# Streaming encoder step with a hierarchical mixture of experts: choices and expert blocks joined into one stage

## The reference: what is computed

```
grp_logits = xt @ w_grp + b_grp                    # 4 groups, xt = rmsnorm(x1)
g_sel      = argmax(grp_logits)                    # one group for each row
e_logits   = xt @ w_exp + b_exp                    # 32 experts, 8 in a group
top_val, top_idx = top_k(e_logits of the group, 2) # two experts for each row
weights    = softmax(grp_logits)[g_sel] * softmax(top_val)
for each chosen expert e:                          # w_e1, w_e3: 1024 x 512, w_e2: 512 x 1024
    h = silu(xb @ w_e1[e]) * (xb @ w_e3[e])
    y += (h @ w_e2[e]) * weight
out = x1 + y
```

## Time and profile before

| | |
|---|---|
| median of three runs | 1229.96 us |
| profiled execution, its own time | 1227.32 us |
| its span, first to last instruction | 1225.5 us |
| busy share of the span: PE, DVE, ACT, POOL | 88%, 35%, 29%, 32% |
| moved by DMA | 289.10 MB, of which queue q1 249.40 MB |
| expert matrices | 96 loads of 2048 KB, median 32.4 us from issue to landing |
| mean granted TensorE clock | 0.956 of full speed |

### The profile page before, as it was taken

The page is one execution under the profiler, slowest core; times in us unless marked ns, Lnnn a source line. Parts: engine busy times, 40 slices in busy tenths (PEclk is TensorE's granted clock), DMA queues, the critical chain, the costliest instruction groups (busy, mean ns, idle before and its releaser), DMA issues. The chain is left out here.

```text
span 1225.5 us, 20512 instructions
## 1 busy us (share of the span) xinstructions
PE 1084.5 (88%) x8243; PEld 832.5 (68%) x8243; DVE 428.3 (35%) x988; ACT 354.5 (29%) x748; POOL 391.2 (32%) x428
## 2 busy tenths in 40 slices
PE   5999899899999989999999896888888888887783
PEld 4998898798999877888898673454445444444441
DVE  6698733891111363342323442211211111111116
ACT  6547633352222644453332431000000000000000
POOL 4454458841211443322554101221212112211100
PEclk9999989898988989999999887999999999999996
DMA  7332236255322531114421898999999999999997
GB/s 130 90 83 70 69 83 167 48 158 130 91 74 61 205 103 38 50 53 139 141 79 44 304 425 354 425 428 424 430 425 429 427 429 427 429 427 430 427 427 264
DMA packets 149678, 289.10 MB, mean 236 GB/s; under 512 B 43668, under 2 KB 119028, under 8 KB 132832
## 3 DMA queue, kind: packets, MB, share of 16 engines
q1 hardware_dynamic: 94224, 249.40, 52.4%
q10 hardware_dynamic: 49632, 27.46, 8.3%
q0 software_dynamic: 5744, 11.15, 2.4%
HBM read 269.30 MB, written 26.54 MB: 241 GB/s over the span
## 5 line engine op out<-in xcount | busy, mean ns | idle before, releaser
L492 PE MATMUL bank<-xhi,cv_w_hi 128*128 128x272 f32 x848 | 260.1, 307 | 9.5 <-PEq L135 3.2
L478 POOL TENSOR_TENSOR cv_w_lo<-cv_w_raw,cv_w_hi 128x1024 fp32r<-128x1024 f32 (+1 forms) x69 | 167.9, 2433 | 310.6 <-ACT cv_w_hi L471 291.8
L2559 PE MATMUL bank<-e_w,b_xT 128*64 128x256 f32 x2048 | 231.0, 383 | 24.4 <-DVE b_xT L2588 14.9
L492 PE MATMUL bank<-xhi,cv_w_lo 128*128 128x272 f32 x848 | 251.2, 296 | 0.0
L492 PE MATMUL bank<-xlo,cv_w_hi 128*128 128x272 f32 x848 | 250.4, 295 | 0.0
L2559 PEld LDWEIGHTS bank<-e_w,b_xT 128*64 128x64 f32 x2048 | 147.3, 138 | 98.0 <-DVE b_xT L2588 19.1
L492 PEld LDWEIGHTS bank<-xhi,cv_w_hi 128*128 128x128 f32 x848 | 165.8, 195 | 18.2 <-issue 10.2
L492 PEld LDWEIGHTS bank<-xlo,cv_w_hi 128*128 128x128 f32 x848 | 166.3, 196 | 0.9
L492 PEld LDWEIGHTS bank<-xhi,cv_w_lo 128*128 128x128 f32 x848 | 165.8, 196 | 0.0
L2571 PE MATMUL bank<-e_w,b_hiddenT 128*64 128x512 f32 x512 | 116.9, 598 | 18.9 <-DVE b_hiddenT L2596 18.9
L2524 POOL COPY b_target<-slot_target 128x1 int32 (+1 forms) x31 | 5.5, 178 | 309.0 <-ACT b_y L2581 288.9
(11 more groups left out here) (447 smaller groups left out, 1641.9 us busy)
## 6 DMA issues: line engine op xcount, KB each, us to landing
e_w<-in_w_e SPq DMA_DIRECT2D x96, 2048.0 KB, 32.4
cv_w_raw<-in_w_in ACTq DMA_DIRECT2D x34, 512.0 KB, 4.2
cv_w_raw<-in_w_in SPq DMA_DIRECT2D x18, 512.0 KB, 3.9
cv_w_raw<-in_w_br_b ACTq DMA_DIRECT2D x8, 512.0 KB, 4.1
o_raw<-in_w_out SPq DMA_DIRECT2D x16, 256.0 KB, 3.7
y_rows<-choice_rows SPq DMA_DIRECT2D x8, 512.0 KB, 11.7
g_values_gates<-g_z_stage ACTq DMA_DIRECT2D x12, 272.0 KB, 4.6
f_gates<-g_values_gates SPq DMA_DIRECT2D x2, 1088.0 KB, 8.7
```

The source lines that it names most:

```text
L478: self.k.nc.gpsimd.tensor_tensor(self.wlo[:, s, 0:nk, :], self.raw[:, s, 0:nk, :], self.whi[:, c % OPS, 0:nk, :].bitcast(F32), ALU.subtract)\
L492: last = self.k.nc.tensor.matmul(self.bank(c, h)[:, 0:HALF], w, x[:, d, cols], start=(d == 0 and n == 0), stop=(d == nk - 1 and n == 2))
L2559: last = nc.tensor.matmul(k.bank[bank][sl[a], 0:FH], xT[:, d, :], w[slot][:, d, FH * a:FH * a + FH], start=(d == 0), stop=(d == KD - 1))
```

## The change

- **One stage.** The two functions now return one function for each engine, and `choices_and_experts` runs both in one block. The barrier between them and the clearing of semaphores there are gone; waits take their place (`picked` when the choices are known, `normed`).
- **Sums in SBUF.** `k.x` keeps its place to the end. The copies to HBM and back (`keep_p`, `keep_s`, `x_back`) are gone. The fourth `w2` buffer, which lay there, is gone as well: eleven matrix buffers, four for `w1`, four for `w3`, three for `w2`.
- **Order of loads.** SP loads `w1` and `w3` of block b and then `w2` of block b - 1. The fourth `w3` buffer holds small tiles of the choices first, so its first load waits for `normed` 5 and `picked`.
- **Turned ahead.** The rows of block b + 1 are turned by PE between the up products of block b and the turning of its gated values, and DVE copies them in two halves around its copy of the gated values. Block 0, block 31 and further blocks turn their own rows.
- **Small moves.** Both clears of `k.xg` stand before the first tile; tile 4's normalised rows have a place of their own, `xn_s`; its store is issued ahead of block 0's gather; DVE works out the targets before it joins block 0's rows; all 31 blocks are written out; the descriptor space of POOL's DMAs is 4096 in place of 8192.

```diff
-RING = 4
+UPS, DOWNS = 4, 3
-k.keep_p, k.keep_s = scratch("sums_prompt", 128, 4, D), scratch("sums_sample", NS, D)
-            k.run(project_and_choose)
-            k.routing.close()
-            k.run(expert_blocks)
+            k.run(choices_and_experts)
...
 SP, choices
             sp.wait_ge(projected, 2)
             load_weights(k, sp, "w_e1", k.w1, k.w1_loaded, 2, 2)
-            sp.wait_ge(added1, 2)
-            sp.dma_start(k.keep_p[:, 0:2, :], k.x[:, 1:3, :]).then_inc(k.x_kept, 16)
             sp.wait_ge(projected, 4)
             load_weights(k, sp, "w_e3", k.w3, k.w3_loaded, 2, 2)
-            sp.wait_ge(added1, 4)
-            sp.dma_start(k.keep_p[:, 2:4, :], k.x[:, 3:5, :]).then_inc(k.x_kept, 16)
             sp.wait_ge(projected, 5)
             load_down(k, sp, 2, 2)
             load_weights(k, sp, "w_e1", k.w1, k.w1_loaded, 3, 3)
-            sp.wait_ge(added1, 5)
-            sp.dma_start(k.keep_s, k.x[0:NS, 0, :]).then_inc(k.x_kept, 16)
+        sp.wait_ge(k.normed, 5)
+        sp.wait_ge(k.picked, 1)
+        load_weights(k, sp, "w_e3", k.w3, k.w3_loaded, 3, 3)
...
 ACT, choices
         move(0, tiles[0][3], 0, TA)
+        for s in range(PAIRS):
+            clear(s)
         a.wait_ge(based, 1)
...
 SP, expert blocks
-                load_weights(k, sp, "w_e3", k.w3, k.w3_loaded, RING - 1, RING - 1)
-                sp.wait_ge(k.x_kept, 16 * 3)
-                load_down(k, sp, RING - 1, RING - 1)
-                for b in range(RING, 2 * EARLY):
-                    loads(sp, b, b, b % RING, b - RING)
+        for b in range(UPS, NE):
+            loads_up(sp, b, b - UPS, b % UPS)
+            loads_down(sp, b - 1, b - 1 - DOWNS, (b - 1) % DOWNS)
+        loads_down(sp, NE - 1, NE - 1 - DOWNS, (NE - 1) % DOWNS)
...
 PE
         def place_first(pe):
+            pe.wait_ge(k.picked, 1)
+            pe.wait_ge(k.normed, 5)
...
-        def products(pe, b, slot, n, half, m):
-            turn(pe, b, half, m).then_inc(turned, 1)
+        def products(pe, b, u, nu, d2, nd, half, m, own=False, ahead=None):
+            if own:
+                turn(pe, b, half, m).then_inc(turned, 1)
...
                 last.then_inc(made, 1)
+            if ahead is not None:
+                turn(pe, b + 1, *ahead).then_inc(turned, 1)
             pe.wait_ge(hidden, b + 1)
...
 SP, end
         def load_rows(eng):
-            eng.wait_ge(up, NE - 2)
-            eng.dma_start(xr[:, 1:5, :], k.keep_p).then_inc(x_back, 16)
-            eng.dma_start(xr[0:NS, 0, :], k.keep_s).then_inc(x_back, 16)
             eng.wait_ge(all_in, 1)
```

More of the change, by code:

```diff
@@ L2105, in expert_tensors @@
     k.w1, k.w3, k.w2 = [], [], []
[L2106 removed]
+    k.w1_loaded, k.w3_loaded, k.w2_loaded = ([sem(f"{w}_loaded{s}") for s in range(n)]
+                                             for w, n in (("w1", UPS), ("w3", UPS), ("w2", DOWNS)))
     for s in range(2):
@@ new lines, in expert_blocks @@
+    last_rows = k.over("m_last_rows", [128, 5, 128], F32, "e_w1_1")
+    nothing = k.over("b_nothing", [128, D // 2], F32, "c_xn", 2 * D)
+    ohw = T("last_weight", 2, 5)
+    other = k.over("m_other", [128, 2 * SLOTS], F32, "c_xn", past)
+    b1, cmpj, ejf = T("blk_oh", 10, MORE), k.over("m_cmpj", [128, MORE, NE], F32, "c_xn"), T("ejf", MORE)
+    names = ("index", "turned", "copied", "first", "up", "silu", "hidden", "hturned", "hcopied", "down", "out")
+    index, turned, copied, first, up, silu, hidden, hturned, hcopied, down, out = (k.sem("b_" + n) for n in names)
@@ L2584, in vector_part, with scalar_part, columns @@
+    def scalar_part(a, b, u, nu, d2, nd, half, m, own=False, ahead=None):
+        a.wait_ge(first, b + 1)
+        wait(a, hidden, b)
+        nc.scalar.activation(act[:], k.bank[1][:, 0:FH], ACT.Silu).then_inc(silu, 1)
+        a.wait_ge(down, b + 1)
+        wait(a, stored, 16 * b)
+        nc.scalar.activation(y[:], k.bank[4][:], ACT.Copy).then_inc(out, 1)
+    def columns(v, b, a):
+        if a == 0:
             v.wait_ge(turned, b + 1)
             wait(v, up, b)
-            for a in range(2):
-                f = slice(4 * a, 4 * a + 4)
-                nc.vector.tensor_tensor(xT[:, f], X[a][:, 0:4 * SLOTS].rearrange("p (k s) -> p k s", k=4),
-                                        k.gain[:, f].unsqueeze(2).broadcast_to([128, 4, SLOTS]), ALU.mult).then_inc(copied, 1)
@@ new lines, in on_gpsimd @@
+    def on_gpsimd(g):
+        g.wait_ge(k.picked, 1)
+        g.wait_ge(k.last_tabled, 16)
+        g.indirect_dma_start(out=xg[:, 1, :], out_offset=None, in_=k.halves,
+                             in_offset=bass.IndirectOffsetOnAxis(ap=k.idx[:, 1:2], axis=0),
+                             bounds_check=2 * NT - 1, oob_is_err=False).then_inc(gathered[1], 16)
+        g.wait_ge(targets, 1)
+        for b in range(NE - 1):
+            if b + PAIRS < NE:
+                fetch(g, b + PAIRS, b % PAIRS, b // PAIRS + 1, b)
+            scatter(g, b, b)
+            if b == 8:
@@ new lines, in expert_blocks, with choices_and_experts, _ @@
+    return on_sync, on_gpsimd, on_scalar, on_tensor, on_vector
+def choices_and_experts(k):
+    choices, experts = project_and_choose(k), expert_blocks(k)
+    with k.nc.Block() as block:
+        @block.sync
+        def _(sp):
+            choices[0](sp)
+            experts[0](sp)
+        @block.gpsimd
+        def _(g):
+            choices[1](g)
+            experts[1](g)
+        @block.scalar
+        def _(a):
+            choices[2](a)
+            experts[2](a)
+        @block.tensor
+        def _(pe):
+            choices[3](pe)
+            experts[3](pe)
+        @block.vector
+        def _(v):
+            choices[4](v)
+            experts[4](v)
```

1146 lines of the change are left out of this document (555 added, 591 removed).

## The result

| | median us | lowest to highest | runs |
|---|---|---|---|
| before | 1227.34 | 1221.29 to 1231.91 | 20 |
| changed | 1232.93 | 1226.51 to 1239.58 | 20 |

The ratio of the times is 1.004, 95% interval 1.0025 to 1.0055: some 5 us slower, clear of noise, but inside the 0.5% that I had set as "the same". The forecast was 1235. The profiled execution of the changed kernel took 1234.48 us, with a span of 1232.6.

A forecast was written before the change was run, and what follows sets the result against it. The prediction took the stream of expert matrices at 427 GB/s as the bound. With `y_rows` flowing 5.3 us later in all, boundary's +1.5 included, span 1225.5 became 1230.8, plus 1.8 made 1232.6, plus 2.6 gave 1235 us; range 1229 to 1241.

The forecast's parts named there:

- Bytes do not pay; the boundary decides: Before block 0: the saved copy out is spent on a longer dip, some 11 us for 4.7, with eleven buffers full.
- the gap is under 6 us: Sign of a wrong prediction: the stream's gap near 745 to 756, expected at 10 to 12 us, is under 6.
- The clears, +0.9: In the choices: both clears before ACT's first tile delay it by 0.9 us, bounds 0 and +1.3.
- Gather, silu, resumption at 738.2, 753.9, 755.5: At block 0: gather issued at 738.2, first silu at 753.9, the stream's data again at 755.5, against 749.1 before.
- Last matrix +1.5: At the stream's end: `w2` of block 31 lands 1.5 us later, at 1196.3.
- Turning ahead: nothing: Between blocks: 1.1 us a block leaves PE's path, but the stream's 14.7 us for three matrices hides it.
- Three `w2` buffers: nothing: Between blocks: loads of `w2` wait for an earlier down product, but up to eight matrices, 39 us, stand ahead; no cost.
- Block 30's down product +11.7, scatter 1196.8: At the end: `w2` of block 30 comes only 4.9 us before the last matrix; product 11.7 us later, scatter at 1196.8.
- Scatter's landing 6.4, bounds from 2.5: At the end: the last scatter lands 6.4 us after issue, bounds 2.5 to 7.4, so `y_rows` flow at 1205.0.
- Block 31 "is not late: DVE comes to its share after ten additions": At the end: block 31 ends near 1210, in time, since DVE needs its share only near 1221.
- the short landing: Rival: gather 1.6 us and last scatter 3.9 us shorter outside the stream, 1229 us, no change; chance 0.16.
- POOL's wait for descriptor space: Rival: each fetch waits for the scatter's landing, POOL's round 17.7 us against 14.7, 90 us more, 1320 us; chance 0.06.

The follow-up runs named there:

- noahead: The changed kernel without turning the next block's rows ahead; every block turns its own rows first. Ratio to the kernel before 1.0014.
- order: The changed kernel with `w2` of block 30 loaded ahead of `w1` and `w3` of block 31. Ratio to the kernel before 1.0025.
- the switches: Two variants of the changed kernel: from block 28 or 16 on, `w2` of b loads right behind its `w1`, `w3`. Ratios to before 0.9977 (28), 0.9994 (16).
- Short: The changed kernel with block 31's up products over half the depth, 32 of 64 matmuls left out. Ratio to the kernel before 1.0026.
- Late: The kernel before, with only its last loads (blocks 30 and 31) in the changed kernel's order. Ratio 1.0037, +4.5 us.
- copies: The changed kernel with the three copies of the sums out to memory put back, not read back. Ratio to the kernel before 1.0071.
- gate: The changed kernel, with SP holding `w2` of block 2 and the load behind it until the fifth tile's root. Ratio to the kernel before 1.0026.

## Why the prediction was right, point by point

- **Bytes do not pay; the boundary decides.** Right in the end, not in the picture. Eleven full buffers waited for the first up product. But the stream first stood idle for 4.3 us at 728 to 740, which I had not foreseen, and the second gap was 5.6 us in place of 10 to 12. The prediction had named "the gap is under 6 us" as a sign of being wrong, and by that sign it was: the moment of resumption came true, the single gap did not.
- **The clears, +0.9.** On ACT the first tile is 1.0 later, as computed. What became of it, the noise of R hides. Not settled.
- **Gather, silu, resumption at 738.2, 753.9, 755.5.** Measured, on that scale: 738.3, 753.4, and about 754.7.
- **Last matrix +1.5.** Undersized: w2 of 31 was issued at 1169.23 and took 31.5, so 1197.5 on the scale of before, +2.7, although the stream resumed some 0.8 earlier than forecast. About 1.0 of these 2.0 is the rate, 426 against 427 over 85 matrices of 2.10 MB; the rest I did not isolate.
- **Turning ahead: nothing. Three `w2` buffers: nothing.** The first is shown by noahead. The second was right in that the queue never ran dry: SP did wait for a down product ahead of each late `w2` load, up to 12.2 us, but even the last one, issued as block 28's down product ended, had 31.5 us to its landing. But the new order of loads moved each `w2` two matrices back in the stream, and I costed that for block 30 alone. It makes every down product from block 11 to block 30 wait, which order (little use) and the switches (6 to 8 us back) show.
- **Block 30's down product +11.7, scatter 1196.8.** Measured +13.0 and 1198.1; the excess is the last matrix's.
- **Scatter's landing 6.4, bounds from 2.5.** Measured 2.7, at the floor. Beside the stream it is longer: the median of the 31 is 7.8. The Trainium skill, page "DMA: Bandwidth & Descriptors", section "Anatomy of one DMA — SWDGE (gpsimd) path", gives about 2.0 us plus the bytes at 436 GB/s, an estimate of 2.6 us for the 262 KB of a scatter; this trace agrees for the one that ran behind the stream, and not for the others. The 15.6 that the earlier trace rows give as the slowest is of a load of `y_rows`, which that view takes in as well: the 31 scatters before took 6.4 to 9.0, median 7.8. The bounds of the gather did not rest on it.
- **Block 31 "is not late: DVE comes to its share after ten additions".** This step failed. On DVE the additions stand *behind* block 31's vector part, so all of block 31's up products (7.1 us) lie between block 30's down product and the first addition. By my sum `y_rows` would flow at 1205.0 and the first addition start 2.5 later, at 1207.5. Measured, on the same scale: the scatter 1.3 later than foreseen, its landing 3.7 shorter, so that the addition could start at 1205.1; DVE came to it at 1206.9, 1.8 later. The errors nearly cancel. Short takes this wait away and gains 2.2 at the first addition of its trace. Late shows that the loads' order alone costs about as much as the whole change; there too the first addition stands directly behind DVE's copy.

So the total (+5.3 foreseen, +3.9 in the profile, +4.9 by the ratio) was right in part by luck: the cause, a late `w2` of block 30, was right, but not the way by which it reached the end. The forecast of 1235 itself stood on three runs of the kernel before with a median of 1229.96; over twenty runs it is 1227.34, and that accounts for the 2.1 by which the measured 1232.93 lies below the forecast. Of the rivals, the short landing came true at the scatter and not at the gather, yet did not bring back "no change". POOL's wait for descriptor space did not appear: its idle before its 32 writes to `choice_rows` is 17.5 us in all, 0.5 each.

Open: why R falls into about 75 or about 78 to 79 in executions of the same code, what the clears and the copies cost in it, and why the kernel without the turning ahead ran 3 us faster, if it did.

## What to carry to other kernels

When loads are reordered or buffers taken away, follow the *consumer* of each moved load in every block, and then what stands behind it in the order of each engine: an engine kept behind a stream cost nothing here until the last block, where all of it came due. Where a ring of buffers fills before its first consumer runs, idle time of the stream ahead of that moment cost nothing behind it in these traces: shorten the way to the first consumer, and keep bulk loads out of the way of the small transfers on it. If a compute chain is faster than the stream, choose the loads' order for prefetch at the start and for earliest finish at the end.

## What the runs showed of the hardware that I had not expected

- Small transfers pay for the stream beside them: block 0's gather took 3.5 us with it held back, 5.4 to 8.5 beside it; the last scatter, from its issue to POOL's release, 2.7 to 3.7 behind or close to the stream's end, 6.5 to 7.5 beside it.
- A stream ends slowly. The changed kernel's last 8 us of weights, by stretches of the windows view, do not run at 427:

```profile
1192.00:1194.00 2.00, 1.43 (x13) 0.83 (x8) 0.42 (x1) 0.00 (x0) 0.00 (x0) 1.00 0.89 367
1194.00:1196.00 2.00, 0.24 (x4) 0.11 (x4) 0.42 (x1) 0.00 (x0) 0.00 (x0) 1.00 0.83 350
1196.00:1198.00 2.00, 2.00 (x10) 0.81 (x12) 0.00 (x0) 0.00 (x0) 0.00 (x0) 1.00 0.48 201
1198.00:1200.00 2.00, 2.00 (x12) 0.80 (x9) 0.00 (x0) 0.38 (x1) 0.00 (x0) 1.00 0.28 111
```

  Until 1200 they lack 3.2 us of full rate. Before, the copy back stood behind the last matrix and filled this. The last matrix is not late by it: it landed 4.9 us behind the one ahead of it (1195.83, 1200.69), the same distance as in the full stream (1180.75, 1185.61).
- The clock. From 770 to 1150 the granted clock was 1.00 before, where PE never waited more than 1.2 us at a time, and 0.96 in the changed kernel. There the down products behind waits of 2.7 to 4.9 us took 5.35 or 5.43 us, those behind waits of 1.6 to 2.2 took 3.65. Two of them, block 27's behind 3.98 us, with 0.57 granted on the mean of the stretch, and block 28's behind 2.19, with 1.00:

```profile
1150.00:1154.00 4.00, 3.99 (x12) 1.52 (x14) 0.00 (x0) 0.00 (x0) 0.00 (x0) 0.57 0.99 420
1165.00:1169.00 4.00, 3.46 (x17) 1.44 (x19) 1.97 (x7) 0.00 (x0) 0.00 (x0) 1.00 1.02 435
```

  The wait alone does not decide: in copies and gate block 30's product took 5.08 and 5.24 us behind 1.76 and 1.58, and A is 15.6 and 15.8 in these two traces, so at the end this can lie on the path.
